# Three modulation products moved ahead, first layer norm folded into the modulation, extra expert blocks nested, last statistics on ScalarE

## What is computed

```python
def adaln(c, ada_w, ada_b):
    mod = jax.nn.silu(c) @ ada_w + ada_b
    return [m[:, None, :] for m in jnp.split(mod, 6, axis=-1)]

def layer_norm(x, g, b):
    mu = jnp.mean(xf, -1, keepdims=True)
    var = jnp.mean(jnp.square(xf - mu), -1, keepdims=True)
    return ((xf - mu) * lax.rsqrt(var + LN_EPS) * g + b).astype(x.dtype)

def trunk_layer(x, c, gla_s0, k_cache, v_cache, slopes, p):
    sh1, sc1, gt1, sh2, sc2, gt2 = adaln(c, ada_w, ada_b)
    h = x * (1 + sc1) + sh1
    gq, gk, gv, gr, loga, sq, sk, sv = in_proj(h, w_in, a2_w, a2_b)
    ...
    mix = mixer_out(o_gla, gr, gla_norm_w, o_swa, w_o, x.dtype)
    x = layer_norm(DEEPNORM_ALPHA * x + gt1 * mix, ln1_g, ln1_b)
    h2 = x * (1 + sc2) + sh2
    x = layer_norm(DEEPNORM_ALPHA * x + gt2 * hier_moe(h2, ...), ln2_g, ln2_b)
```

## Time and profile before

| | us |
|---|---|
| median of 3 executions | 743.1 |
| lowest and highest | 741.85 and 743.35 |
| the profiled execution, its time | 743.77 |
| the profiled execution, its span | 741.5 |
| granted TensorE clock, mean of the span | 0.894 |

### The profile page before, as it was taken

One profiled execution on the slowest core, in us unless ns is written; L12 is line 12 of the kernel. 1 busy time (PEld: TensorE's weight loads), 2 busy tenths in 40 slices (PEclk: granted clock), 3 DMA queues, 4 the chain that ended last, 5 costly groups with the idle time before them and its releaser, 6 DMA issues.

```text
span 741.5 us, 10794 instructions
## 1 busy us (share of the span) xinstructions
PE 617.3 (83%) x4458; PEld 392.8 (53%) x4458; DVE 327.8 (44%) x592; ACT 135.0 (18%) x356; POOL 103.2 (14%) x144
## 2 busy tenths in 40 slices
PE   3679999899998798999754999888888878878494
PEld 2459999676765564454443655444444444435241
DVE  2463361655524552375675245433333333343248
ACT  1442351334343053011120100000000000000100
POOL 3000000100001202000012233322222222222100
PEclk9979999999998587999955899988999999989797
DMA  8981330003009798501499599999999999996243
GB/s 301 369 220 58 66 114 2 14 1 114 1 3 383 257 384 213 197 29 42 170 364 356 196 408 408 408 405 407 406 408 408 408 400 398 402 399 267 77 187 117
DMA packets 75899, 181.03 MB, mean 244 GB/s; under 512 B 22164, under 2 KB 26108, under 8 KB 75844
## 3 DMA queue, kind: packets, MB, share of 16 engines
q1 hardware_dynamic: 65220, 163.39, 59.5%
q0 software_dynamic: 7936, 14.09, 5.5%
q10 hardware_dynamic: 2688, 2.77, 1.1%
HBM read 176.25 MB, written 14.45 MB: 257 GB/s over the span
## 4 chain that ended last, share of the span: by engine, by line
PE 48%; SPq 25%; DVE 11%; DMA 8%; issue 4%; ACT 3%; DVEq 0%; ACTq 0%; POOLq 0%
SPq L431 24%; PE bank L941 9%; PE bank L1175 7%; PE bank L1279 6%; PE bank L1008 6%; PE bank L1297 3%; DMA ring<-in_moe_w_up_dram 3%; DMA ring<-in_ada_w_dram 2%; PE bank L895 2%; PE bank L990 2%; DMA x_tok<-in_x_sample_dram 2%; PE bank L1138 1%; PE bank L1061 1%; PE bank L1142 1%; PE bank L1032 1%
## 5 line engine op out<-in xcount | busy, mean ns | idle before, releaser
L1279 PE MATMUL bank<-late_w,xT 128*64 128x256 f32 x672 | 88.5, 423 | 19.8 <-DMA late_w<-in_moe_w_up_dram 15.9
L1279 PEld LDWEIGHTS bank<-late_w,xT 128*64 128x64 f32 x672 | 55.1, 152 | 59.3 <-DMA late_w<-in_moe_w_up_dram 26.5
L1279 PE MATMUL bank<-ring,xT 128*64 128x256 f32 x480 | 65.6, 435 | 16.9 <-DMA ring<-in_moe_w_up_dram 15.1
L1759 DVE COPY xT<-bank 128x512 f32<-128x512 f32 x36 | 24.7, 692 | 124.1 <-PE bank L1265 123.7
L1279 PEld LDWEIGHTS bank<-ring,xT 128*64 128x64 f32 x480 | 39.6, 157 | 47.2 <-DMA ring<-in_moe_w_up_dram 23.9
L838 ACT ACTIVATE sgl<-bank 128x128 f32<-128x128 f32 x36 | 10.0, 278 | 250.0 <-PE bank L1279 250.0
L601 POOL DMA_INDIRECT expert_rows<-ye,dsti x36 | 36.6, 1016 | 125.1 <-DVE ye L1778 125.1
L594 POOL DMA_INDIRECT xg<-h_scratch,srci x38 | 38.9, 1025 | 105.7 <-PE bank L1265 94.1
L1775 DVE SCALAR_TENSOR_TENSOR S<-bank,modrt,S 128x512 f32<-128x512 f32 x36 | 27.0, 751 | 37.3 <-PE bank L1297 37.3
L1297 PE MATMUL bank<-late_w,hT 128*64 128x512 f32 x168 | 40.7, 604 | 1.2 <-issue 1.2
L1008 PE MATMUL bank<-ring_r,h_high 128*128 128x512 f32 (+1 forms) x140 | 38.4, 415 | 0.0
(11 more groups left out here) (309 smaller groups left out, 883.3 us busy)
## 6 DMA issues: line engine op xcount, KB each, us to landing
ring<-in_ada_w_dram SPq DMA_DIRECT2D x22, 1024.0 KB, 10.3
late_w<-in_moe_w_gate_dram SPq DMA_DIRECT2D x21, 1024.0 KB, 16.5
late_w<-in_moe_w_up_dram SPq DMA_DIRECT2D x21, 1024.0 KB, 20.1
late_w<-in_moe_w_down_dram SPq DMA_DIRECT2D x21, 1024.0 KB, 19.9
ring<-in_moe_w_down_dram SPq DMA_DIRECT2D x15, 1024.0 KB, 20.1
ring<-in_moe_w_gate_dram SPq DMA_DIRECT2D x15, 1024.0 KB, 16.4
ring<-in_moe_w_up_dram SPq DMA_DIRECT2D x15, 1024.0 KB, 20.2
ring<-in_w_in_dram SPq DMA_DIRECT2D x7, 1024.0 KB, 6.0
```

The source lines that it names most:

```text
L1279: mm = pe.matmul(bank[2 + a][f * C:(f + 1) * C, 0:2 * P], x, w[:, kk, f, :, :], start=(kk == 0), stop=(kk == KD - 1))
```

## The change

In four parts, none of which changes what is computed:

1. **Early pairs.** The weights of modulation pairs 4 to 6 no longer pass through the ring. They go, 2 MB at a time, to two tiles in `areaC` that are free until the v projection writes there. The three pairs share these tiles. Pair 4 is issued just ahead of sq0, pair 5 ahead of kv, pair 6 ahead of gv1, each after the former pair has been used. PE runs pair 4 after `tb` 6, pair 5 after `tb` 8, pair 6 after the transposing of the cached keys. `ADA_STATE` goes.
2. **Joined norm.** `joined` makes one scale row and one shift row per group of rows from ln1 and the modulation, once for the prompt and once for the sample. `h2` then takes two operations after the subtraction of the mean instead of four. The row x itself, which only the last norm needs, gets its scale and shift later (`x_scale`, `x_shift`). The load of expert 4 now waits for x (`x_norm`), since its slot lies over the ln1 rows.
3. **Nested extra pairs.** The `If`s stand inside each other, so that the first one not taken leaves them all. The rows of the next pair are transposed within the pair before, ahead of `down`.
4. **Last norm.** ACT takes row sums and sums of squares from PSUM with `accum_out`; DVE makes the mean and adds the two halves of the squares.

```diff
+        EARLY_AT = {number[("sq0", 0)]: 0, number[("kv", 0)]: 1, number[("gv1", 0)]: 2}
...
                     sp.wait_ge(*freed(former(n)))
+                if n in EARLY_AT:
+                    i = EARLY_AT[n]
+                    if i >= 1:
+                        sp.wait_ge(pe_mod, NPAIR1 + i)
+                    for b in range(2):
+                        sp.dma_start(early_tiles[b].rearrange("p (k n) -> p k n", k=KD // 2),
+                                     ada_half(NA1 + 2 * i + b)).then_inc(s_early[i], 16)
...
-                        sp.wait_ge(*((pe_y, NT), (h2_ready, NP), (h2_ready, NT))[e - 2])
+                        sp.wait_ge(*((pe_y, NT), (h2_ready, NP), (x_norm, NT))[e - 2])
...
                     proj_t(tb, unit_parts(q), slice(b * P, (b + 1) * P)).then_inc(pe_t, 1)
                     tb += 1
+                ada(NPAIR1 + q - 2, 3 + q - 2)
...
             pe.transpose(bank[1][:, 0:WIN], kc[:, :], ident[:, :]).then_inc(pe_t, 1)
+            pe.wait_ge(z_ev, 10)
+            ada(NPAIR1 + 2, 0)
...
-                if j in ADA_STATE:
-                    p = ADA_STATE[j]
-                    pe.wait_ge(tok_ev, len(TOK)) if j < 2 else pe.wait_ge(ada_ev, p - 1)
-                    ada(p, 3 + p % 2)
...
+            for b in (E, E + 1):
+                turn_x(b % 2, 16 * (b // 2 + 1), b - 1)
+            pe.wait_ge(xe_ev, E + 2)
+            with ExitStack() as taken:
+                for i in range(NOV // 2):
+                    taken.enter_context(pe.If(pairs > i))
...
                     for b in (E + 2 * i, E + 2 * i + 1):
                         turn_h(b % 2, b + 1, b)
+                        if b + 2 < NBLK:
+                            turn_x(b % 2, 16 * ((b + 2) // 2 + 1), b + 1)
                         down(b % 2, b % R, 16 * (b // R + 1), b + 1, b - 1)
+                    pe.wait_ge(xe_ev, min(E + 2 * i + 4, NBLK))
...
+            def joined(md, r):
+                link(dve.scalar_tensor_tensor(ytmp[0:r, :], md[2][0:r, :], 1.0, ln1[0:r, 1, :], ALU.add, ALU.mult))
+                link(dve.tensor_tensor(md[1][0:r, :], md[1][0:r, :], ytmp[0:r, :], ALU.add))
+                link(dve.scalar_tensor_tensor(md[2][0:r, :], md[2][0:r, :], 1.0, ln1[0:r, 0, :], ALU.add, ALU.mult))
...
-                link(dve.scalar_tensor_tensor(h2[0:r, j % 2, :], md[2][0:r, :], 1.0, x, ALU.add, ALU.mult))
+                link(dve.tensor_tensor(h2[0:r, j % 2, :], x, md[2][0:r, :], ALU.mult))
                 dve.tensor_tensor(h2[0:r, j % 2, :], h2[0:r, j % 2, :], md[1][0:r, :], ALU.add).then_inc(h2_ready, 1)
+                if j < NP - 1:
+                    x_scale(j)
+                    x_shift(j)
...
+            row_sums(0)
+            row_sums(1)
+            row_squares(0)
             for j in range(NT):
...
+                if j + 2 < NT:
+                    row_sums(j + 2)
+                row_std(j)
+                if j + 1 < NT:
+                    row_squares(j + 1)
```

More of the change, by code:

```diff
@@ L615, in _ @@
                     scatter(e - 2, e % 2)
-            for i in range(NOV // 2):
-                with pool.If(pairs > i):
+            with ExitStack() as taken:
+                for i in range(NOV // 2):
+                    taken.enter_context(pool.If(pairs > i))
                     for b in (E + 2 * i, E + 2 * i + 1):
@@ L1738, in _ @@
             link(dve.tensor_copy(dsti[:, :], ent[:, :]))
+            x_scale(NP)
+            x_shift(NP)
             dve.wait_ge(pe_wtb, 1)
```

174 lines of the change are left out of this document (105 added, 69 removed).

## The result

| | us |
|---|---|
| before, median of 5 (lowest to highest) | 743.1 (741.85 to 745.26) |
| changed, median of 5 | 749.23 (746.79 to 752.25) |
| ratio | 1.0068 (95% interval 1.0042 to 1.0094) |
| profiled execution, its time and span | 746.79 and 745.1 |
| ratio of a second measurement, 12 executions (`change_again`) | 1.0069 (1.0039 to 1.0100) |

The change makes the kernel clearly slower, by 5 us by the ratio and 6 by the medians, where 744.0 was forecast, 0.9 more than before; 749.2 lies over the range. The profiled execution was the lowest of the five, 3.0 above that of before, so the two profiles show only 3 of these us. Executions of one kernel lie up to 10 us apart here, more than I allowed for.

What follows compares the result with a forecast made beforehand. The DMA-bound expert weight stream was taken as the limit, so only time before the first expert and the tail count. +5.2 - 4.0 - 2.6 + 0.2 + 2.1 = +0.9 gave 744.0 us against the 743.1 median; range 738.5 to 748.0.

Steps and rivals of the forecast that it cites:

- the exit's 4.0: After the last expert: with one exit from the skipped `If`s, PE starts on rows read back 4.0 us sooner, at 706.0.
- the clock's loss behind the kv wait: Projection: after PE's 3.1 us wait before `proj_t(9)`, products run slowly at a lower clock, adding 1.5 us.
- early pairs: Projection and state stage: 6.9 of moved products, 3.1 of waiting, 1.5 of lost clock, less 6.3 in state stage: +5.2 us.
- joined norm and first gather: Routing up to the first expert: shorter way to h2 (-4.0) and quieter landing of the first gathered rows (-2.6): -6.6 us.
- nested pairs and tail: Extra expert pairs (+0.2) and everything behind the last block, including the last norm (+2.1): +2.3 us.
- My own sign: Routing: PE's transposing of block 4's h2 starts near 380.5; off by over 1.5, one of the first two parts is wrong.
- Joined norm: Ahead of routing: two DVE operations of 1.23 fewer before each h2 bring block 4 forward: -4.0 us.
- pair 11: Between blocks 3 and 4: this modulation pair's products on PE become the limit, ending at 375.6 instead of 378.1.
- First gather: Before expert 0: with expert 4's loads held back, the gathered rows land in about 4.0 instead of 6.6: -2.6 us.
- Nested pairs: Extra expert pairs: saved idle time is offset by waits, so the last `gated_rows` ends where it did: +0.2 us.
- Tail: Behind the last block: one exit starts additions sooner, but the norm's longer chain over ACT and DVE ends later: +2.1 us.
- slow 1: At the end: one exit costs PE as much as six skips, adding 5.0 instead of 2.1: 746.9 us, chance 0.20.

Runs made afterwards that it cites:

- `change_again`: The changed kernel, unaltered, measured once more in twelve executions: ratio to the kernel before 1.0069, median 749.52 us against 743.5.
- `joined_only`: The kernel before with the joined norm alone, including the load of expert 4 waiting for x: ratio to the kernel before 0.9895.
- `expert4_later`: The kernel before with expert 4's three loads waiting for the slots' weights, so issued behind the first gather: ratio to the kernel before 0.9978.
- `no_early`: The changed kernel with modulation pairs 4 to 6 back in the ring and the state stage: ratio to the kernel before 0.9988.
- `kv_first`: The changed kernel with the kv load issued ahead of pair 5's two loads in SyncE's queue: ratio to the kernel before 0.9993.
- `nest_only`: The kernel before with the nested extra pairs alone and the old last norm: ratio to the kernel before 0.9974.

## Why the prediction was wrong, by its steps

**Two steps failed.** One is that PE's additions in the tail would run as fast as before, so that the exit's 4.0 would remain. The other is the size of the clock's loss behind the kv wait. The table sets the prediction's terms beside the first profile and beside the ratios of the kernels with and without each part. Each ratio is uncertain by some 2 us, and each difference of two ratios by some 3.

| term | forecast | first profile | by the ratios |
|---|---|---|---|
| early pairs | +5.2 | +8.05 | +6.0 (1.0069 less 0.9988) |
| joined norm and first gather | -6.6 | -7.3 | -7.8 (0.9895) |
| nested pairs and tail | +2.3 | +2.7 | +6.9 (0.9988 less 0.9895) |

**Early pairs: +5.2 forecast, +8.05 in the profile, 6.0 by the ratios.** The mechanism was right: kv behind pair 5, the weights there at 107.4 (forecast 106.6), a wait of 3.49 (3.1). Mis-sized was the clock behind it: 1.5 forecast, 2.84 measured (6.69 against 3.85). I had taken the loss of one row for the whole loss of a low stretch. About 0.5 more of the lateness was there already when pair 4 began (94.28, where `tb` 7 began at 93.76 before). The state stage gave back 5.7 and not 6.3. In all four profiles with this order PE is 8.05 to 9.9 late at the stage's end. My own sign, block 4's transposing within 1.5 of 380.5, failed at 382.86 and points here.

**Joined norm: -4.0 forecast, -4.4 measured**, and -5.0 without the early pairs. The size is right. In the change the limit between blocks 3 and 4 was DVE (2.71 of waiting), not pair 11 on PE; in `joined_only` it was PE, as predicted.

**First gather: -2.6 forecast, -2.65 measured.** Right, and `expert4_later` shows the reason. The stretch I called idle for expert 4's loads was not so at its start (DMA share 0.78 from 404 to 408 before), but the loads cost nothing: see the next line.

**Nested pairs: +0.2 forecast.** From expert 0's `gate_up` to the last scatter it is as long as before (288.4), so this was right.

**Tail: +2.1 forecast, +2.7 in the first profile** (742.63 - 739.09, less the 0.81 by which the last scatter was late), +6.1 in that of `change_again`, and with other parts than forecast. The exit was right, -4.1 at the start of the additions. From there to the end 6.1 more were reckoned; it was 7.6 here and 9.2 in `change_again`. The step that failed is that the additions would run as fast as before: those of block 4 were to take 5.2 and took 8.4. Before, PE's low stretch fell on the 7.34 of adding x, ahead of anything that was awaited. With the exit the additions of x are nearly as slow (7.11), and a second low stretch falls on additions that DVE waits for. The nest gained 1.9 alone and nothing behind the joined norm, where 4 were reckoned at the start of the additions. The order on ACT cost most of the rest, and the sum had it (the root behind `row_sums(4)`). The sum also had a slip: its terms put the first root's end near 719.5 and not at 720.5 (719.36 in the trace), which hid 1 us of the loss.

**The sum** came to +0.9. The span of the first profile is 3.6 longer than that of before, and there the early pairs are the term that is most off, by 2.85. By the ratios the whole is +5.1, and the term most off is the tail with the nest, by 4.6. In the four profiles with the nest and this norm (the first one, `change_again`, `no_early`, `kv_first`) it is +1.8 to +6.1 from the last scatter to DVE's end, so that it looked right in the first one was luck. Which of the two terms weighs more in a typical execution stays open. My range had each rival alone, never two, and nothing for the scatter of the executions. The rival whose time is nearest, slow 1 at 746.9, had the wrong reason: PE did not start late on the rows read back. Its idle time over the skipped code fell from 8.80 to 2.78, and lay ahead of the rows' landing. It goes with what the Trainium skill, "Runtime: NRT & Kernel Launch", section "Instruction fetch mechanics", has on branches to code that isn't fetched, though one exit costs more than a sixth of six. That this fetch is the cause, no run here shows.

## What to carry over

Before a load is put into a queue ahead of another, ask which engine converts or evacuates something behind the second one, in its own order: 12 us of ACT's waiting came from one load that was put behind 2 MB. Where an engine serves several blocks in turn, what finishes an old block belongs ahead of what begins one whose input isn't there. A wait of TensorE ahead of long work can cost nearly twice its length (3.49 waited, 2.84 lost behind it), though not each does (2.69 waited, 0.1 lost). Where a kernel scatters by 1% between executions, rank edits by stage lengths from several profiles and by the ratio, not by one profile's total.

## What the runs showed that I had not expected

- TensorE's clock fell to its lower level for some 3 to 7 us at a time also where the engine was 98% to 100% busy (granted 0.64 and 0.68 in 65 to 75 of `kv_first`, 0.66 in 125 to 130 of `change_again`), in some profiles and not in others, and also without any part of the change ahead of it: `nest_only`, which differs from before only behind the 32 experts, has 0.71 in 65 to 70 (95% busy), where before has 1.00. What brings this about is open.
- An fp32 product of 512 columns is two passes: eight fillers were 16 entries and took 7.03, so 0.44 a pass.
- A load of a function table on ACT delayed the next instruction by its own 1.28 and nothing more (717.78 to 719.07).
- Loads issued 0.8 and 0.4 us ahead of a gather held it up as much as loads issued 14 to 18 us ahead of it (PE waited 4.7 and 4.6 for the rows).
